# The gates of one token block added in DRAM by index

## The chip, the cores and the metric

The kernel runs on one core of one Trainium2 chip. Its engines are TensorE (PE, with its weight loads shown as PEld), VectorE (DVE), ScalarE (ACT), GpSimd (POOL) and SyncE (SP); 16 DMA engines move data between DRAM and the on-chip memory, and SP, ACT and POOL issue transfers to them on a queue each. The metric is the device time of one execution in microseconds (us), smaller is better.

## The reference

One transformer layer for 1024 tokens of width 1024. The first half is a gated mixer and its projections. The second half is PEER: every token picks 16 of 16384 experts in each of 8 heads, by the best 16 sums of two key scores, and adds up those experts' rows.

```
i1, i2: places of the 16 best scores of each half (128 keys each)
idx   = i1 * 128 + i2 of the 16 best sums
gate  = softmax(top_s)                          # per token and head, 16 numbers
act   = gelu(expert_u[idx] . h)
y     = sum over heads and choices of gate * act * expert_v[idx]
```

Nothing of what is computed changes here.

## The kernel before

The 1024 tokens are eight blocks of 128. Blocks 0 to 2 are stream A, blocks 3 to 7 are stream B (`NT` = 640 tokens). Stream A computes PEER **sparsely**: POOL gathers for each of 384 slots (block, head, choice) the 128 rows that the 128 tokens name, once from `expert_u` and once from `expert_v`, 512 KB each (line 746), and DVE takes a dot product (`u_row`, line 1139) or adds the weighted row (`v_row`, line 1148). These 768 gathers are listed in `ROWS`, spread over the units of stream B's work, and each goes to a row buffer of a small ring (`BUFFERS`); a gather waits until DVE has used the row that was in its buffer.

Stream B computes PEER **densely**, in units that run in the order of the table `UNITS`:

- 64 **E units** (`E`,0 to 63; 128 x 2 experts each in two feature tiles): PE multiplies the unit of `expert_u` with the 640 tokens, 96 matmuls of 320 columns, since every value is split in a high and a low half-precision part; ACT applies gelu and stores the result in DRAM (`a_dram`, line 990). ACT and DVE convert the next weight units (`make_hi`, line 753; `make_lo`, line 1043); DVE also ranks stream B's scores in units 0 to 35 and takes gathered rows.
- 64 **W units**, two for each of 32 groups: SP reads back `a_dram` and the gates `g_dram` (`load_group`), DVE multiplies them (`product`, line 1510), splits the product, and PE multiplies with `expert_v`.

The gates must lie densely for the product: for each token a 128 x 128 matrix over (i1, i2), mostly zero. **Spreading** makes it: beside each of the 20 E units from `E_SPREAD` = 40 to 59, for 32 tokens a unit in 8 steps of 4 tokens, DVE builds one-hot matrices (`onehot_keys`, line 1496, and `onehot_gate`, line 1503), PE multiplies them (8 matmuls of 128 columns a step, line 1925), ACT copies the outcome and stores 2 MB to `g_dram` (line 986). Ahead of it stand, on DVE, `shift_scores` in unit 35 and `gates` in unit 37; the index matrices are transposed on PE and copied out by ACT in units 38 and 39 (`index_tiles`, `indices_out`); `idx_t` closes unit 39 on DVE, **behind** that unit's gathered rows. From then on PE's next step waits on DVE, four steps at most apart.

In the loop over `UNITS` POOL, ACT, DVE and PE each work in program order. A gather's two ends are the semaphores `row_in` (landed) and `row_used` (taken by DVE). ACT's `gelu_dots` waits for the dots of two sections before. DVE's `make_lo` in an E unit that doesn't spread waits for the ACT conversion that follows this same unit's evacuation.

Of the kernel before, what the change touches and what calls it, by code (L numbers as in the profile page):

```python
# [45 lines left out]
HB = NT // 2  # L46
NGRP = 32
# [128 lines left out]
X_G = X_IDX + 6  # L176
X_END = X_G + NT // 4

# [12 lines left out]
N_SPREAD = NT // 32  # L191
E_SPREAD = 2 * NGRP - N_SPREAD - 4

# [105 lines left out]
def trunk_layer(nc, x, c_row, w_cond, b_col, w_front, ln_g, ln_b, w_spat, b_spat, conv_w,  # L299
                ln1_g, ln1_b, keys_t, u_units, v_units, u_rows, v_rows, ln2_g, ln2_b, out):  # L300
    with ExitStack() as ctx:
# [38 lines left out]
        idx_sp = sb("idx_sp", [P, SLOTS], U32)  # L340

# [94 lines left out]
        keys_t16 = zone(15300, 640, F16).rearrange("p (n c t) -> p n c t", c=2, t=2)  # L436
        gates16 = zone(15940, 640, F16).rearrange("p (n c t) -> p n c t", c=2, t=2)
        g_t = zone(16580, 640)
# [9 lines left out]
        G_t = [z.rearrange("p (n h j t) -> p n h j t", n=NT // 32, h=2, j=4) for z in (zone(5120, 5120), hB_flat)]  # L448
# [17 lines left out]
        g_dram = nc.dram_tensor("g_dram", [NGRP // 2, P, NT // 32, 2 * P], F32).ap()  # L466
# [22 lines left out]
        row_in = [sem(f"row_in{i}") for i in range(18)]  # L489
        end_in = sem("end_in")  # L490
# [72 lines left out]
        def _(sp):  # L563
# [152 lines left out]
        def _(pool):  # L716
# [4 lines left out]
            pool.iota(iota_i[:, :], pattern=[[1, P]], base=0, channel_multiplier=0).then_inc(ident_ready, 1)  # L721
            for i in range(2):
                pool.wait_ge(ws_in, 16 * (i + 1))
                pool.memset(ws_t[64:P, :, 0:64], 0.0).then_inc(mask_ready, 1)
# [5 lines left out]
            for m, (table, slot, _) in enumerate(ROWS):  # L730
# [20 lines left out]
        def _(act):  # L751
# [76 lines left out]
            def indices_out(lo, hi):  # L828

                for i in range(lo, hi):  # L830
                    kind, (first, last) = i // 2, SPLIT["B"][i % 2]
                    a = X_IDX + i
                    n, at = (last - first) * P, slice(first * P, last * P)
                    wait_x(act, a)
                    if kind < 2:
                        pairs = slice(first * P // 2, last * P // 2)
                        activation(keys_t16[:, pairs, kind, :], psX[a % 4][:, 0:n].rearrange("p (n t) -> p n t", t=2)
                                   ).then_inc(x_free[a % 4], 1)
                    else:
                        activation(g_t[:, at], psX[a % 4][:, 0:n], ACT.Copy, GS).then_inc(x_free[a % 4], 1)  # L840
# [23 lines left out]
            for n, (x, kind, u) in enumerate(UNITS):  # L864
# [69 lines left out]
                elif kind == "E":  # L934
# [18 lines left out]
                    for j in range(2):  # L953
                        for half in range(2):
# [3 lines left out]
                            if u == E_SPREAD - 1 and 2 * j + half == 1:  # L958
                                indices_out(4, 6)
# [18 lines left out]
                if (x, kind, u) == ("B", "E", E_SPREAD - 2):  # L978
                    act.wait_ge(row_used, RANK_ROWS)
                    indices_out(0, 4)  # L980
# [14 lines left out]
                if (x, kind, u) == ("B", "E", E_SPREAD - 4):  # L995
# [31 lines left out]
        def _(dve):  # L1027
# [160 lines left out]
            dve.wait_ge(ident_ready, 2)  # L1188
# [282 lines left out]

            ranks = {}
# [7 lines left out]
            def idx_t():  # L1480
                for i in range(4):
                    a = X_IDX + 5 - i
# [22 lines left out]
            def product(g):  # L1505
                dve.wait_ge(a_in[g % 2], 16 * (g // 2 + 1))
                dve.wait_ge(g_in[g // 2 % 2], 16 * (g // 4 + 1))
                for j in range(4):
                    a = A_t[g % 2][:, j, :].rearrange("p (n t) -> p n t", n=NT // 32)
                    ins = V.scalar_tensor_tensor(a, a, AS, G_t[g // 2 % 2][:, :, g % 2, j, :], ALU.mult, ALU.mult)  # L1510
                    if j < 3:
                        step(ins)
                    else:
                        settle()
                        ins.then_inc(prod_ready, 1)
# [11 lines left out]
            for n, unit in enumerate(UNITS):  # L1527
# [69 lines left out]
                elif kind == "E" and u < E_SPREAD - 4:  # L1597
# [110 lines left out]
        def _(pe):  # L1708
# [140 lines left out]
            def index_tiles(lo, hi):  # L1849

                for i in range(lo, hi):
                    flat = (i1_all, i2_all, s_all)[i // 2]["B"].rearrange("p b h k -> p b (h k)")
                    first, last = SPLIT["B"][i % 2]
                    ps = x_tile(X_IDX + i)
                    for b in range(first, last):
                        ins = nc.tensor.transpose(ps[:, (b - first) * P:(b - first + 1) * P], flat[:, b, :], ident[:, :])
# [6 lines left out]
            for n, (x, kind, u) in enumerate(UNITS):  # L1863
# [66 lines left out]
                elif (x, kind, u) == ("B", "E", E_SPREAD - 1):  # L1930
                    def gates_between(r, s):
                        if (r, s) == (1, 2):
                            pe.wait_ge(gate_ready, 2)
                            index_tiles(4, 6)
# [5 lines left out]
                if (x, kind, u) == ("B", "E", E_SPREAD - 2):  # L1940
                    pe.wait_ge(s_shift, 2)
                    index_tiles(0, 4)
# [85 lines left out]
```

## Time and profile before

| | us |
|---|---|
| median of 3 runs | 2945.51 |
| lowest and highest run | 2930.32, 2946.67 |
| span of the profiled execution | 2939.3 |
| PE, DVE, ACT, POOL busy in it | 2830.0, 2512.5, 885.5, 1029.0 |

The profiled execution is told by its span, from the first instruction to the last; its own time outside the profile is not listed, and the span lies between the lowest run and the median. A busy share over the whole span mixes stages with different limits. The E units of this trace begin near 1060 us, spreading is from 1691 to 2036 us, the W units run from about 2110 us. Granted clock 1.00 means 2.4 GHz.

### The profile page before, as it was taken

Reading aid. Unit: us, or ns where it says so; the run is one execution under the profiler, and the core shown is the slowest. Engines: PE = TensorE matmul, PEld = TensorE weight load, DVE = VectorE, ACT = ScalarE, POOL = GpSimd, SP = SyncE. Lnnn points to the kernel's source line nnn. Section 1 sums busy time; section 2 is a strip of 40 time slices with the busy share of each in tenths; the row PEclk is TensorE's granted clock in tenths of the full one; section 3 lists DMA queues with packets and bytes.
Section 4 is the critical chain, followed back from the end, with each engine's and each line's share of the span. In section 5 each row is a group of like instructions: output and inputs, shape, how many; then the busy total and the mean of one; then the engine's idle time right before and its main releaser. Section 6 shows DMA issues by size and latency. Waiting matters only on the chain. (4 is left out here: it accounts for less than half of the span.)

```text
span 2939.3 us, 47358 instructions
## 1 busy us (share of the span) xinstructions
PE 2830.0 (96%) x19184; PEld 1834.9 (62%) x19184; DVE 2512.5 (85%) x4708; ACT 885.5 (30%) x1321; POOL 1029.0 (35%) x778
## 2 busy tenths in 40 slices
PE   4999999998999999999999999999999999999998
PEld 4566686766667877677776677777544444444443
DVE  6876556987887879999999999998699999999877
ACT  3333532221111432222222344444222222222223
POOL 0000000002776025444554532222456566655410
PEclk9999999999999999999999999999999999999999
DMA  8989653433999458888888999999999999999972
GB/s 328 348 318 381 238 199 129 144 123 115 391 392 378 192 215 288 303 325 314 330 315 320 354 327 346 350 346 341 368 398 405 405 388 414 407 401 404 364 267 115
DMA packets 222971, 917.54 MB, mean 312 GB/s; under 512 B 20208, under 2 KB 61216, under 8 KB 181536
## 3 DMA queue, kind: packets, MB, share of 16 engines
q1 hardware_dynamic: 61664, 427.91, 37.3%
q0 software_dynamic: 110592, 402.70, 36.4%
q10 hardware_dynamic: 50496, 83.89, 7.9%
q8 instruction: 152, 2.49, 0.3%
q14 instruction: 67, 0.55, 0.1%
HBM read 771.79 MB, written 142.63 MB: 311 GB/s over the span
## 5 line engine op out<-in xcount | busy, mean ns | idle before, releaser
L1718 PE MATMUL psU<-hB,w 128*128 128x320 f16 (+2 forms) x3104 | 927.4, 299 | 27.4 <-ACT Z L753 15.9
L1719 PE MATMUL psU<-hB,w 128*128 128x320 f16 (+2 forms) x3104 | 927.3, 299 | 0.0
L1720 PE MATMUL psU<-hB,w 128*128 128x320 f16 (+2 forms) x3104 | 927.0, 299 | 0.0
L753 ACT ACTIVATE w<-stage 128x2048 f16<-128x2048 f32 x176 | 335.7, 1909 | 606.1 <-PE psX L1720 331.2
L1043 DVE SCALAR_TENSOR_TENSOR w<-stage,w 128x2048 f16<-128x2048 f32 x176 | 402.3, 2287 | 99.4 <-ACT w L753 99.4
L746 POOL DMA_INDIRECT rows<-in_u_rows,idx_sp x200 | 267.8, 1339 | 376.0 <-DVE rows L1139 233.5
L1718 PEld LDWEIGHTS psU<-hB,w 128*128 128x128 f16 x3104 | 304.9, 98 | 140.2 <-issue 22.9
L1720 PEld LDWEIGHTS psU<-hB,w 128*128 128x128 f16 x3104 | 305.1, 98 | 117.6
L1719 PEld LDWEIGHTS psU<-hB,w 128*128 128x128 f16 x3104 | 305.0, 98 | 110.4
L746 POOL DMA_INDIRECT rows<-in_v_rows,idx_sp x205 | 271.4, 1324 | 285.4 <-DVE rows L1139 184.5
L1718 PE MATMUL psX<-w,Z 128*128 128x512 f16 x768 | 292.2, 381 | 7.6 <-DVE Z L1641 4.2
L1719 PE MATMUL psX<-w,Z 128*128 128x512 f16 x768 | 292.6, 381 | 0.0
L1720 PE MATMUL psX<-w,Z 128*128 128x512 f16 x768 | 292.5, 381 | 0.0
L1148 DVE SCALAR_TENSOR_TENSOR acc_sp<-rows,weight_sp,acc_sp 128x1024 f32<-128x1024 f32 x205 | 258.3, 1288 | 30.5 <-DMA rows<-in_v_rows,idx_sp 26.2
L1718 PE MATMUL psU<-w,Z 128*128 128x512 f16 (+1 forms) x768 | 265.1, 345 | 5.4 <-ACT acc_sp L753 2.8
L1139 DVE SCALAR_TENSOR_TENSOR rows<-rows,h_sp 128x1024 f32<-128x1024 f32 x200 | 239.6, 1220 | 29.8 <-DMA rows<-in_u_rows,idx_sp 28.9
L1719 PE MATMUL psU<-w,Z 128*128 128x512 f16 (+1 forms) x768 | 265.1, 345 | 0.0
L1720 PE MATMUL psU<-w,Z 128*128 128x512 f16 (+1 forms) x768 | 265.0, 345 | 0.0
L753 ACT ACTIVATE R<-psU 128x320 f32<-128x320 f32 (+1 forms) x296 | 123.1, 427 | 333.6 <-PE psU L1720 333.3
L753 ACT ACTIVATE Z<-psU 128x320 f32<-128x320 f32 (+3 forms) x228 | 97.0, 445 | 383.6 <-PE psU L1720 341.6
L1718 PE MATMUL psU<-Z,w 128*128 128x384 f16 (+1 forms) x640 | 206.5, 323 | 5.6 <-DVE w L1043 5.6
L1720 PE MATMUL psU<-Z,w 128*128 128x384 f16 (+1 forms) x640 | 206.8, 323 | 0.0
(263 smaller groups left out, 4435.8 us busy)
## 6 DMA issues: line engine op xcount, KB each, us to landing
stage<-in_u_units SPq DMA_DIRECT2D x64, 1024.0 KB, 8.8
stage<-in_v_units SPq DMA_DIRECT2D x64, 1024.0 KB, 8.0
stage<-in_w_front SPq DMA_DIRECT2D x48, 1024.0 KB, 8.6
hl_dram<-w SPq DMA_DIRECT2D x48, 1024.0 KB, 6.5
w<-hl_dram SPq DMA_DIRECT2D x48, 1024.0 KB, 7.2
a_dram<-R ACTq DMA_DIRECT2D x64, 640.0 KB, 8.0
g_dram<-Z ACTq DMA_DIRECT2D x20, 2048.0 KB, 10.7
Z<-a_dram SPq DMA_DIRECT2D x32, 1280.0 KB, 11.8
```

The costliest lines, as they stand in the source:

```text
L746: pool.indirect_dma_start(row_at[r], None, u_rows if table == "u" else v_rows, bass.IndirectOffsetOnAxis(ap=idx_sp[:, slot:slot + 1], axis ...
L753: return nc.scalar.activation(dst, src, func, scale=scale)
L1043: V.scalar_tensor_tensor(w[:, n % NW, 1, :], stage[:, v % 2, :], WS, w[:, n % NW, 0, :], ALU.mult, ALU.subtract).then_inc(lo_done, 1)
L1139: V.scalar_tensor_tensor(row_at[r], row_at[r], 1.0, h2_sp[:, slot % SB, :], ALU.mult, ALU.mult, accum_out=dots[:, c % 8, j:j + 1]).then_in ...
L1148: V.scalar_tensor_tensor(dst, row_at[r], weight_sp[:, slot:slot + 1], dst, ALU.mult, ALU.add).then_inc(row_used, 1)
L1718: mm(ps, lhs[0](k), rhs[0](k), start=start and s == 0, stop=False)
L1719: mm(ps, lhs[0](k), rhs[1](k), start=False, stop=False)
L1720: last = mm(ps, lhs[1](k), rhs[0](k), start=False, stop=stop and s == n - 1)
```

## The change

Block 7, the last of stream B (`DS` = 1), is taken out of the spreading. Its gates go to a second DRAM tensor, `gs_dram` (16384 x 128 numbers, 8 MB), which is first filled with zeros: POOL clears one row buffer at the start, and ACT issues 16 transfers of 512 KB from it, one beside each of the 16 units from (`B`,`V`,2) on. When `gates` is through, DVE works out in `scatter_slots` where each gate of block 7 goes, and POOL adds the gates there: one indirect DMA with an add for each of 8 heads x 16 choices, each for 128 tokens with one number of 4 bytes a token, 128 DMAs. They stand two ahead of each gathered row, beginning with unit 38's rows; ahead of each head's 16 POOL waits until all adds before have landed, as two heads can name the same expert.

The spreading holds 512 tokens in 16 E units, 44 to 59 (`E_SPREAD` = 44); the units 40 to 43 are plain. Rank, `shift_scores` and `gates` stay where they were (`E_RANK` = 36). As `_sections` goes by `E_SPREAD - 4`, units 37 and 39 take 3 + 3 gathered rows where they took 2 + 2, and two slots leave the W units. The transposed index tiles are 3 of 512 columns where they were 6. Each pair of W groups reads 2 MB of `g_dram` and 512 KB of `gs_dram`, the latter in 1024 pieces of 512 bytes; `product` is four operations of 512 columns and one of 4 x 128.

```diff
+DS = 1
+DV = DB - DS
+NV = DV * P
+TS = DS * P
...
-N_SPREAD = NT // 32
+N_SPREAD = NV // 32
 E_SPREAD = 2 * NGRP - N_SPREAD - 4
+E_RANK = 36
+ZERO_FIRST, ZERO_N = N_OF["B", "V", 2], 16
+N_SCATTER = DS * HEADS * TOPK
+SCATTER_FIRST, SCATTER_LAST = E_RANK + 2, 2 * NGRP - 6
...
+                    sp.dma_start(G_s[pair % 2].rearrange("p h j t -> p (h j) t"), gs_dram[pair]
+                                 ).then_inc(g_in[pair % 2], 16)
...
+            sp.wait_ge(gs_added, 16 * N_SCATTER)
             load_group(0)
...
+            def add_gates(n):
+
+                for _ in range(min(n, N_SCATTER - added[0])):
+                    i = added[0]
+                    if i == 0:
+                        pool.wait_ge(scatter_ready, 1)
+                    elif i % (DS * TOPK) == 0:
+                        pool.wait_ge(gs_added, 16 * i)
+                    pool.indirect_dma_start(gs_flat, bass.IndirectOffsetOnAxis(ap=at_s[:, i:i + 1], axis=0),
+                                            gate_s[:, i:i + 1], None, compute_op=ALU.add).then_inc(gs_added, 16)
+                    added[0] += 1
+
+            pool.wait_ge(gs_zeroed, 16 * ZERO_N)
+            for m, (table, slot, c) in enumerate(ROWS):
+                _, kind, u = SEC_UNITS[c]
+                if kind == "E" and SCATTER_FIRST <= u < SCATTER_LAST:
+                    add_gates(2)
...
+                if ZERO_FIRST <= n < ZERO_FIRST + ZERO_N:
+                    if n == ZERO_FIRST:
+                        act.wait_ge(zeros_ready, 1)
+                    part = gs_zero[n - ZERO_FIRST]
+                    act.dma_start(part, zeros.unsqueeze(1).to_broadcast([P, part.shape[1], D])).then_inc(gs_zeroed, 16)
...
+            def scatter_slots():
+
+                for b in range(DS):
+                    i1, i2 = (t["B"][:, DV + b].rearrange("p h k -> p (h k)") for t in (i1_all, i2_all))
+                    step(V.tensor_scalar(i1, i1, float(TS), tok[:, b:b + 1], ALU.mult, ALU.add))
+                    settle()
+                    step(V.scalar_tensor_tensor(i2, i2, float(P * TS), i1, ALU.mult, ALU.add))
+                    settle()
+                    at = at_s[:, b * P:(b + 1) * P]
...
+                        V.tensor_copy(at, i2).then_inc(scatter_ready, 1)
...
-                dve.wait_ge(g_in[g // 2 % 2], 16 * (g // 4 + 1))
+                dve.wait_ge(g_in[g // 2 % 2], 32 * (g // 4 + 1))
                 for j in range(4):
-                    a = A_t[g % 2][:, j, :].rearrange("p (n t) -> p n t", n=NT // 32)
-                    ins = V.scalar_tensor_tensor(a, a, AS, G_t[g // 2 % 2][:, :, g % 2, j, :], ALU.mult, ALU.mult)
...
+                    a = A_t[g % 2][:, j, 0:NV].rearrange("p (n t) -> p n t", t=32)
+                    step(V.scalar_tensor_tensor(a, a, AS, G_t[g // 2 % 2][:, :, g % 2, j, :], ALU.mult, ALU.mult))
+                a = A_t[g % 2][:, :, NV:NT]
+                ins = V.scalar_tensor_tensor(a, a, AS, G_s[g // 2 % 2][:, g % 2], ALU.mult, ALU.mult)
...
-                elif kind == "E" and u < E_SPREAD - 4:
+                elif kind == "E" and u < E_RANK:
...
-                if kind == "E" and u == E_SPREAD - 5:
+                if kind == "E" and u == E_RANK - 1:
                     rank_some("B", 7, 9)
                     shift_scores("B")
-                if kind == "E" and u == E_SPREAD - 3:
+                if kind == "E" and u == E_RANK + 1:
                     gates("B", 2)
+                    scatter_slots()
```

POOL's order at unit 38, before (each row a gather; `in_u_rows` and `in_v_rows` are the expert tables, in brackets the semaphores waited for):

```order
L746 DMA Z<-in_u_rows,idx_sp 128x1024 [waits x_ready]
L746 DMA rows<-in_u_rows,idx_sp 128x1024 [waits row_used]
L746 DMA rows<-in_v_rows,idx_sp 128x1024 [waits row_used] x2
L746 DMA rows<-in_u_rows,idx_sp 128x1024 [waits row_used]
L746 DMA Z<-in_u_rows,idx_sp 128x1024 [waits row_used]
```

and in the changed kernel, from unit 38's first row to the first wait for the adds:

```order
L768 DMA gs_dram<-Z 2097152x1 [waits scatter_ready]
L768 DMA gs_dram<-Z 2097152x1
L792 DMA Z<-in_u_rows,idx_sp 128x1024 [waits row_used]
L768 DMA gs_dram<-Z 2097152x1 x2
L792 DMA rows<-in_u_rows,idx_sp 128x1024 [waits row_used]
L768 DMA gs_dram<-Z 2097152x1 x2
L792 DMA rows<-in_v_rows,idx_sp 128x1024 [waits row_used]
...
L768 DMA gs_dram<-Z 2097152x1 [waits gs_added]
L768 DMA gs_dram<-Z 2097152x1
L792 DMA rows<-in_v_rows,idx_sp 128x1024 [waits row_used]
```

Line 768 is the add, line 792 the gather. Where POOL issued one DMA a gathered row it now issues three, for 64 rows, and seven times one of them waits for the landing of those before.

DVE's order in unit 37 and at the start of unit 38, changed kernel (line 1508 to 1512 are `gates`, 1187 a dot, 1196 a weighted row):

```order
L1512 TENSOR_TENSOR Z<-Z 128x640 [waits dve_step]
L1525 TENSOR_SCALAR Z<-Z,tok 128x128 [waits gate_ready]
L1527 SCALAR_TENSOR_TENSOR Z<-Z 128x128 [waits dve_step]
L1533 CAST Z<-Z 128x128 [waits dve_step]
L1187 SCALAR_TENSOR_TENSOR rows,dots<-rows,h_sp 128x1024 [waits row_in2]
L1187 SCALAR_TENSOR_TENSOR rows,dots<-rows,h_sp 128x1024 [waits row_in3]
L1187 SCALAR_TENSOR_TENSOR rows,dots<-rows,h_sp 128x1024 [waits row_in0]
L1196 SCALAR_TENSOR_TENSOR acc_sp<-rows,weight_sp,acc_sp 128x1024 [waits row_used,row_in1,weight_ready]
```

The three operations of `scatter_slots` stand ahead of the unit's rows; the unit has a third dot and a third weighted row.

## Rows read from the trace of the kernel before

**Rows 1.** The page: busy time, and the span in 40 slices.

```profile
PE 2830.0 (96%) x19184; PEld 1834.9 (62%) x19184; DVE 2512.5 (85%) x4708; ACT 885.5 (30%) x1321; POOL 1029.0 (35%) x778
...
POOL 0000000002776025444554532222456566655410
...
DMA  8989653433999458888888999999999999999972
```

**Rows 2.** Windows: stretch, length, busy us (instructions) by engine, clock, DMA share, GB/s.

```profile
1600.00:1700.00 100.00, 90.98 (x653) 64.98 (x654) 92.89 (x166) 34.26 (x58) 53.67 (x40) 0.93 0.87 326
1700.00:1800.00 100.00, 99.31 (x942) 75.79 (x941) 99.20 (x144) 45.48 (x82) 30.18 (x26) 1.00 0.97 351
```

**Rows 3.** Tile `g_dram`: ACT's stores, duration ns, first and last start.

```profile
L986 ACTq DMA_DIRECT2D g_dram<-Z x20: 377/377/380, 1710.7 to 2035.6; - x20
```

**Rows 4.** Timeline of ACT, units 60 to 63: start, length, stores of `a_dram`.

```profile
2049.11 0.33 ACTq L990 DMA_DIRECT2D a_dram<-R  x1
...
2088.03 0.33 ACTq L990 DMA_DIRECT2D a_dram<-R  x1
```

**Rows 5.** Groups by form, DVE, 1700 to 2050 us: count, busy us, mean ns, idle before.

```profile
L1503 DVE TENSOR_TENSOR Z<-Z 128x1024 f16<-128x1024 f16 x156 | 107.4, 688 | 2.7
L1496 DVE TENSOR_TENSOR Z<-Z 128x1024 f16<-128x1024 f16 x155 | 106.0, 684 | 0.0
L1043 DVE SCALAR_TENSOR_TENSOR w<-stage,w 128x2048 f16<-128x2048 f32 x20 | 45.7, 2283 | 3.9 <-ACT w L753 3.9
L1148 DVE SCALAR_TENSOR_TENSOR acc_sp<-rows,weight_sp,acc_sp 128x1024 f32<-128x1024 f32 x28 | 35.7, 1279 | 0.0
L1139 DVE SCALAR_TENSOR_TENSOR rows<-rows,h_sp 128x1024 f32<-128x1024 f32 x28 | 34.1, 1218 | 0.0
```

**Rows 6.** Timeline of DVE at the end of unit 39.

```profile
1685.03 1.23 DVE L1139 SCALAR_TENSOR_TENSOR rows<-rows,h_sp 128x1024 f32<-128x1024 f32 x1 [3.21 <-DMA rows<-in_u_rows,idx_sp]
...
1689.93 0.48 DVE L1485 CAST Z<-Z 128x640 f16<-128x640 f32 x1
```

**Rows 7.** Timeline of PE at the first step of the spreading.

```profile
1692.99 1.04 PE L1925 MATMUL psX<-Z 128*128 128x128 f16 x8 [6.65 <-DVE Z L1503]
```

**Rows 8.** Timeline of POOL, plain units, then spreading: start, length, idle before.

```profile
1601.61 1.68 POOL L746 DMA_INDIRECT Z<-in_u_rows,idx_sp  x1 [13.84 <-DVE Z L1139]
1603.59 0.94 POOL L746 DMA_INDIRECT Z<-in_v_rows,idx_sp  x1 [0.30 <-issue]
...
1608.56 1.89 POOL L746 DMA_INDIRECT rows<-in_u_rows,idx_sp  x1 [0.31 <-issue]
...
1725.61 1.14 POOL L746 DMA_INDIRECT rows<-in_u_rows,idx_sp  x1 [2.58 <-DVE acc_sp L1148]
```

**Rows 9.** Waits, 1500 to 2060 us: total, times, longest.

```profile
POOL rows L746 <- DVE rows L1139: 116.1, 37, 13.5
POOL rows L746 <- DVE acc_sp L1148: 95.7, 29, 4.8
```

**Rows 10.** Tile `rows`, 1600 to 1700 us: time from issue to landing.

```profile
DMA to landing us min/median/max: 5.3/8.9/13.5
```

**Rows 11.** Tile `rows`, 1700 to 2050 us: the same.

```profile
DMA to landing us min/median/max: 4.5/8.2/11.9
```

**Rows 12.** The page: DMA queues, packets, MB, share of 16 engines.

```profile
q0 software_dynamic: 110592, 402.70, 36.4%
q10 hardware_dynamic: 50496, 83.89, 7.9%
```

**Rows 13.** Windows of the zero fill's units and of the W units.

```profile
440.00:540.00 100.00, 100.00 (x707) 69.55 (x706) 71.99 (x266) 25.70 (x46) 0.00 (x0) 1.00 0.40 137
540.00:620.00 80.00, 80.00 (x578) 56.99 (x577) 75.14 (x336) 22.13 (x38) 0.00 (x0) 1.00 0.30 107
...
2200.00:2300.00 100.00, 100.00 (x465) 45.25 (x464) 95.97 (x105) 24.81 (x16) 65.07 (x43) 1.00 1.00 403
```

**Rows 14.** Groups by form, 1700 to 2400 us: `product` of the W units.

```profile
L1510 DVE SCALAR_TENSOR_TENSOR Z<-Z 128x640 f32<-128x640 f32 x28 | 21.1, 815 | 13.1 <-DMA Z<-g_dram 13.1
```

More of the change, by code:

```diff
@@ L434, in trunk_layer @@
         a_ring = v3(R1[:, :], 4)
-        keys_t16 = zone(15300, 640, F16).rearrange("p (n c t) -> p n c t", c=2, t=2)
-        gates16 = zone(15940, 640, F16).rearrange("p (n c t) -> p n c t", c=2, t=2)
-        g_t = zone(16580, 640)
+        keys_t16 = zone(15300, NV, F16).rearrange("p (n c t) -> p n c t", c=2, t=2)
+        gates16 = zone(15940, NV, F16).rearrange("p (n c t) -> p n c t", c=2, t=2)
+        g_t = zone(16580, NV)
+        at_s = zone(R2 + 13968 + NV, TS, U32)
+        gate_s = zone(R2 + 14608 + NV, TS)
+        zeros = rows[:, 3, :]
         iota_k2 = v3(zone(17220, 128, F16), P)
@@ L446, in trunk_layer @@
         A_t = [v3(zone(2560 * i, 2560), 4) for i in range(2)]
-        G_t = [z.rearrange("p (n h j t) -> p n h j t", n=NT // 32, h=2, j=4) for z in (zone(5120, 5120), hB_flat)]
+        G_t = [z[:, 0:8 * NV].rearrange("p (n h j t) -> p n h j t", n=NV // 32, h=2, j=4)
+               for z in (zone(5120, 5120), hB_flat)]
+        G_s = [z[:, 8 * NV:8 * NT].rearrange("p (h j t) -> p h j t", h=2, j=4) for z in (zone(5120, 5120), hB_flat)]
         c_hi = [v3(zone(10240 + 1280 * i, 1280, F16), 4) for i in range(2)]
@@ L489, in trunk_layer @@
         row_in = [sem(f"row_in{i}") for i in range(18)]
+        zeros_ready = sem("zeros_ready")
+        gs_zeroed = sem("gs_zeroed")
+        gs_added = sem("gs_added")
+        scatter_ready = sem("scatter_ready")
         end_in = sem("end_in")
@@ L721, in _ @@
             pool.iota(iota_i[:, :], pattern=[[1, P]], base=0, channel_multiplier=0).then_inc(ident_ready, 1)
+            pool.iota(tok_i[:, :], pattern=[[P, DS]], base=0, channel_multiplier=1).then_inc(ident_ready, 1)
+            pool.memset(zeros, 0.0).then_inc(zeros_ready, 1)
+            pool.wait_ge(zeros_ready, 1)
             for i in range(2):
@@ L729, in _ @@
             pool.memset(acc_sp[:, :, :], 0.0).then_inc(acc_zeroed, 1)
-            for m, (table, slot, _) in enumerate(ROWS):
+            added = [0]
+            def add_gates(n):
[13 more added lines that the diff above has]
+                    add_gates(2)
                 r, before, _ = PLACES[m]
@@ L828, in indices_out @@
             def indices_out(lo, hi):
[L830 to L833, printed above, removed]
+                for kind in range(lo, hi):
+                    a = X_IDX + kind
                     wait_x(act, a)
                     if kind < 2:
-                        pairs = slice(first * P // 2, last * P // 2)
-                        activation(keys_t16[:, pairs, kind, :], psX[a % 4][:, 0:n].rearrange("p (n t) -> p n t", t=2)
+                        activation(keys_t16[:, :, kind, :], psX[a % 4][:, 0:NV].rearrange("p (n t) -> p n t", t=2)
                                    ).then_inc(x_free[a % 4], 1)
                     else:
-                        activation(g_t[:, at], psX[a % 4][:, 0:n], ACT.Copy, GS).then_inc(x_free[a % 4], 1)
+                        activation(g_t, psX[a % 4][:, 0:NV], ACT.Copy, GS).then_inc(x_free[a % 4], 1)
             def section_gelu(n):
@@ L1470, in slots_A @@
                 V.tensor_copy(idx_sp[:, :], idx_f).then_inc(slots_ready, 1)
+            def scatter_slots():
[6 more added lines that the diff above has]
+                    at = at_s[:, b * P:(b + 1) * P]
+                    if b < DS - 1:
+                        step(V.tensor_copy(at, i2))
+                    else:
+                        V.tensor_copy(at, i2).then_inc(scatter_ready, 1)
             ranks = {}
@@ L1480, in idx_t @@
             def idx_t():
-                for i in range(4):
-                    a = X_IDX + 5 - i
+                for a in range(X_IDX, X_G):
                     dve.wait_ge(x_free[a % 4], a // 4 + 1)
@@ L1851, in index_tiles @@
                 for i in range(lo, hi):
-                    flat = (i1_all, i2_all, s_all)[i // 2]["B"].rearrange("p b h k -> p b (h k)")
-                    first, last = SPLIT["B"][i % 2]
+                    flat = (i1_all, i2_all, s_all)[i]["B"].rearrange("p b h k -> p b (h k)")
                     ps = x_tile(X_IDX + i)
-                    for b in range(first, last):
-                        ins = nc.tensor.transpose(ps[:, (b - first) * P:(b - first + 1) * P], flat[:, b, :], ident[:, :])
+                    for b in range(DV):
+                        ins = nc.tensor.transpose(ps[:, b * P:(b + 1) * P], flat[:, b, :], ident[:, :])
                     ins.then_inc(x_ready, 1)
```

31 lines of the change are left out of this document (17 added, 14 removed).

## The prediction

> **What bounds the kernel now.** I read the windows by stage first, then the pace of the units, and only then single instructions. Over the whole span PE is busy 96% and DVE 85%, POOL 35% [rows 1]; the share says little about the stretch that the change touches. In the spreading PE and DVE are both busy 99% of each window [rows 2]. ACT stores 20 batches of gates from 1710.7 to 2035.6 [rows 3]: 324.9 / 19 = **17.1 us a spreading unit**. Three plain units behind them take 2088.03 - 2049.11 = 38.9 [rows 4], so **13.0 us a plain unit**, which is PE's own pace. DVE's list for a spreading unit, from the means [rows 5], is 8 x (0.69 + 0.68) + 2.28 + 2 x 1.28 + 2 x 1.22 = 18.2 us by busy times that overlap a little: it fills the 17.1. In a plain unit DVE has only 2.28 + 2.56 + 2.44 = 7.3 us of it.
>
> The other thing to see is the seam. The spreading starts when DVE has taken unit 39's rows and built the first one-hots: DVE waited 3.21 us there for a gathered row and came to `idx_t` at 1689.93 [rows 6], and PE stood 6.65 us [rows 7]. **Whatever makes DVE late before the seam is paid by PE at the seam**, since nothing lies between them there. And DVE is late when gathered rows are. Today POOL waits for DVE (116.1 + 95.7 us over the stretch, for buffers [rows 9]), not DVE for POOL.
>
> **What is taken away.** Four units go from spreading to plain: 4 x (17.1 - 13.0) = **-16.4 us**. Fewer index tiles are copied; they are behind PE's work and cost nothing. This is all that the change can give back, 0.6% of the time.
>
> **What is added on POOL.** 128 adds by index, each for 128 tokens like a gather. No add is in the trace. Its nearest row is the gather: 0.94 us and 0.30 to the next when nothing is waited for, with a longer one of 1.89 closing a run [rows 8]. Five issues after the run's first (0.94 x 4 + 1.89, and 5 x 0.30) make 7.15 us, **1.43 us each**; in the spreading 1.14 + 0.30 = 1.44. I take 1.43 for both kinds, as each makes descriptors for 128 indices. Ends: 0.30, if an add cost nothing but the gap, and 2.19 (1.89 + 0.30), if each was like the longest of the run. Less than nothing is excluded, since nothing leaves POOL's queue.
>
> Seven times POOL also waits until all adds have landed. A gather lands 8.9 us (5.3 to 13.5) after issue in the plain units and 8.2 (4.5 to 11.9) in the spreading [rows 10, 11]. An add stands behind the gather issued just before it, so I take 7 us, less the one gather that POOL still issues between: 7.0 - 1.4 = **5.6 us a wait**; ends 0 and 12 - 1.4 = 10.6. The rule that speaks for less: the Trainium skill, "DMA: Bandwidth & Descriptors", section "Anatomy of one DMA", puts a small transfer at about 2 us to landing, most of it the receipt of the write. By that the seven waits would cost 7 x 0.6, some 35 us less in all. The trace does not agree for this load, as no gather landed in under 4.5 us; 512 KB and the queue before it explain that.
>
> **Plain units 38 to 43.** They take 4, 6, 4, 4, 4, 4 = 26 gathered rows and so 52 adds: 78 issues x 1.43 = 111.5, and three waits (before adds 17, 33 and 49) 16.8, together 128.3 us of POOL. PE needs 6 x 13.0 = 78.0. POOL now gets there **50.3 us late**. Buffers for 5 to 7 rows cannot hide it: DVE uses a row 8 or 9 us after issue at best, and POOL itself can't start until `scatter_ready` in unit 37. I set what the buffers hide against that late start. PE runs on to the seam with weights converted up to four units ahead, and waits there.
>
> **Spreading units 44 to 53.** The other 76 adds with 38 rows, in ten units of 40: 116 x 1.43 = 165.9, and four waits 22.4, are 188.3 us against 10 x 17.1 = 171.0: **+17.3 us**. POOL is then the bound here too, by little. From unit 54 on the queue is as before.
>
> **What else moves, at nothing.** The zero fill, 8 MB, goes out beside work where DMA share is 0.40 and 0.30 [rows 13]; at the gathers' price (36.4% of 2939.3 us for 402.7 MB [rows 12] is 2.66 us a MB) it needs 22 us of some 200 that are free. POOL's memset and ACT's 16 issues wait for nobody. `scatter_slots` is three operations of 128 columns, below 0.69 us each [rows 5], in a unit where DVE's 2.28 + 3 x 1.28 + 3 x 1.22 = 9.8 us leave 3.2 for them and for `gates`. The two extra rows each in units 37 and 39 are in the count above.
>
> In the W units `product` grows from 4 x 0.815 [rows 14] to five operations of 512 columns; with the 0.815 scaled by columns at best, 0.65, it is 3.3 us, at worst 4.1: up to 0.8 us a group. A group is 10 tiles of 12 matmuls and 465 matmuls pass in 100 us [rows 13], so it lasts 25.8 us. DVE is busy 96% and PE 100% there [rows 13], so 1 us a group is about free; cost zero, at worst 32 x 0.8 less that slack, near zero. The DMA side is the thinner cover: share 1.00 at 403 GB/s. The moved 8.4 MB come in 512-byte pieces. ACT's queue, half of it in 1 KB pieces, pays 7.9% of the span for 83.9 MB [rows 12], 2.77 us a MB against 2.66, so I take nothing; if short pieces cost double it is +22 us over 32 groups.
>
> **Sum.** -16.4 + 50.3 + 17.3 = **+51 us**. Against the profiled span, 2939.3, that is 2990; the median of the runs lies 6 us above the span, so the forecast is **2996 us**.
>
> **Rivals.**
> 1. *POOL's idle time takes it all* (the other side: not slower). POOL is idle 65% of the span [rows 1] and 70% of a spreading window [rows 2]. It holds if an issue is so cheap that 52 of them with three waits, beside 26 gathers at 1.43, fit in 78.0: (78.0 - 37.2 - 3w) / 52, which is 0.78 us an add with no wait and 0.46 with the 5.6. Then only -16.4 is left: **2929**. For it: an add moves 4 bytes a token and not 4096. Against it: a gather's 0.94 us on POOL is its issue, not its transfer, which lands 8 us later. The same page of the Trainium skill calls descriptor generation "small, variable", which would put it here; the 0.94 speaks against. Chance 0.2.
> 2. *Adds land slowly.* Each engine must read, add and write 8 single numbers an add. If it does that one after the other, a wait is not 5.6 but 15 us or more, and gathers queued behind adds come late too. 7 x (15 - 5.6) = 66 more: **3062**; with 1.9 us issues (52 + 76 adds x 0.76 = 97 more) about **3160**. Nothing in the trace shows an adding DMA. Chance 0.2.
> 3. *The W units become bound by DMA*, with POOL's cost as in 1: -16.4 + 22 = **2951**. For it: DMA share 1.00; against it: PE never stands. Chance 0.05.
> 4. *The change doesn't do what it says*, if adds stay behind to the last: they'd end by unit 53 or 54 by the count, ten units before `load_group` asks. Chance 0.02.
>
> My forecast has 0.53, as far as from 2960 to 3060.
>
> **Numbers.** A measurement of this kernel tells 1%, some 29 us, from no change. Faster by over 1% would need 13 us more than the change can give: 0.06, out of rival 1's chance, for what I don't see. Within 1%, 2916 to 2975: the rest of rival 1, rival 3, and the forecast's cheap end (issues of 1.24 us and waits of 2.6: -16.4 + 26.5 + 0 = +10 us): 0.27. Slower: 0.67. The range leaves out the far end of rival 2 and little below rival 1: **2926 to 3100**.
>
> **What would show it.** The stretch of spreading has 16 stores at 17 to 19 us. POOL, 50% busy in 1600 to 1700 now, is busy or waiting for its own adds nearly throughout units 38 to 53, and its waits for DVE's buffers vanish there. DVE waits for gathered rows tens of us in all. PE stands at the seam by some 50 us, not 6.65. The W units keep 25.8 us a group. If PE's stand at the seam is below 10 us, the POOL term is wrong; if POOL is idle and still the rows are late, it is the landing.

## The result and the profile after

The change costs 5.5%: **3099.79 us**, median of 6 runs (3086.07 to 3106.52), against 2945.60 (2925.06 to 2947.60) for the kernel before in the same session, a ratio of 1.0546 (1.0511 to 1.0580). The forecast was 2996, +51 us; the measured +154 is three times that, and the time lies 0.2 us inside the upper end of the range, 3100. Of all runs told of here one, of experiment 11, was in the slower state (3003.16 us at a granted clock of 0.942, where the others of its kernel have 0.984 to 0.993) and is left out.

Where the 161.6 us between the two profiled spans lie is read off the starts of ACT's stores to `a_dram`, one an E unit:

| stretch | before | after | difference |
|---|---|---|---|
| start to unit 36 | 1645.7 | 1650.7 | +5.0 |
| unit 36 to 43 (plain units, half of the seam) | 116.7 | 117.7 | +1.0 |
| unit 43 to 44 (rest of the seam) | 17.1 | 80.7 | +63.6 |
| unit 44 to 53 (adds beside the spreading) | 153.9 | 223.9 | +70.0 |
| unit 53 to 63 | 154.7 | 154.4 | -0.3 |
| unit 63 to the end | 851.3 | 873.5 | +22.2 |

A unit's time is counted here from the store before it to its own. The kernel before has its own seam in the second row (unit 40, 25.5 us) and spreads in the units 40 to 59, so the rows compare the whole stretch better than single units. From unit 54 on the pace is 17.1 us a unit again, to the tenth.

The page after: busy time, then POOL's, the clock's and the DMA engines' 40 slices, then POOL's queue.

```profile
PE 2837.4 (92%) x18925; PEld 1827.6 (59%) x18925; DVE 2479.6 (80%) x4680; ACT 867.1 (28%) x1286; POOL 1284.6 (41%) x908
...
POOL 0000000005762144454557878852265656565520
PEclk9999999999999999999999769999999999999999
DMA  8989654337997478888888657889899999999973
...
q0 software_dynamic: 129024, 402.78, 36.4%
```

Against [rows 1] POOL has 130 instructions more and 256 us more of busy time, 7s and 8s in the slices of units 38 to 53; the same slices are where DMA is less busy than before and the clock falls. 128 of the 130 are the adds. They move 0.08 MB in 18432 packets [rows 12].

The windows of the stretch, columns as in [rows 2]:

```profile
1600.00:1700.00 100.00, 92.53 (x664) 65.89 (x665) 84.79 (x180) 32.16 (x51) 62.59 (x43) 0.95 0.83 300
1700.00:1800.00 100.00, 44.28 (x319) 31.39 (x317) 30.70 (x35) 14.71 (x24) 82.47 (x52) 0.73 0.63 158
1800.00:1900.00 100.00, 50.26 (x409) 36.75 (x410) 55.03 (x78) 19.45 (x34) 79.28 (x52) 0.74 0.64 167
```

In 1700 to 1800 every engine but POOL is idle more than half of the time, and POOL's 82.47 us with 52 gaps of 0.30 leave it no more than 2 us of waiting. That is an engine that is full, though its busy share reads 82%. How it fills, from POOL's timeline in the changed kernel:

```profile
1785.14 2.54 POOL L768 DMA_INDIRECT gs_dram<-Z  x1 [0.30 <-issue]
1787.99 1.56 POOL L768 DMA_INDIRECT gs_dram<-Z  x1 [0.30 <-issue]
1789.85 1.01 POOL L792 DMA_INDIRECT rows<-in_u_rows,idx_sp  x1 [0.30 <-issue]
1791.16 1.58 POOL L768 DMA_INDIRECT gs_dram<-Z  x1 [0.30 <-issue]
1793.05 1.56 POOL L768 DMA_INDIRECT gs_dram<-Z  x1 [0.30 <-issue]
1794.91 1.48 POOL L792 DMA_INDIRECT rows<-in_v_rows,idx_sp  x1 [0.30 <-issue]
```

One gathered row now takes two adds of 1.6 and a gather of 1.0 to 1.5, with three gaps: 5.1 us from gather to gather here, and 2 x 2.08 + 1.64 = 5.8 in the mean over the list (an add and a gather with their gaps), where PE's plain units want a row every 13.0 x 6 / 26 = 3.0. The same by groups, POOL, 1500 to 2250 us (count, busy us, mean ns, idle before):

```profile
L768 POOL DMA_INDIRECT gs_dram<-Z x128 | 227.4, 1776 | 45.4 <-issue 37.8 <-DMA gs_dram<-Z 5.2 <-DVE Z L1533 2.4
L792 POOL DMA_INDIRECT rows<-in_u_rows,idx_sp x53 | 70.0, 1320 | 64.2 <-DVE acc_sp L1196 37.6 <-DVE rows L1187 15.9 <-issue 10.7
```

An add takes 1.78 us of POOL and 0.30 to the next. The waits for the landing of adds are 5.2 us in all, in three places; at the other four all had landed when POOL came there. One of the three, the last add of a head, the gather behind it and the add that waits:

```profile
1763.94 1.56 POOL L768 DMA_INDIRECT gs_dram<-Z  x1 [0.30 <-issue]
1765.80 1.01 POOL L792 DMA_INDIRECT rows<-in_u_rows,idx_sp  x1 [0.30 <-issue]
1769.09 1.58 POOL L768 DMA_INDIRECT gs_dram<-Z  x1 [2.28 <-DMA gs_dram<-Z]
```

What the rest of the machine does meanwhile, from the waits of 1600 to 2250 us (total, times, longest):

```profile
ACT Z L799 <- PE psX L1986: 254.2, 100, 59.4
PEld psX L1986 <- DVE Z L1565: 130.5, 34, 67.6
PE psX L1986 <- DVE Z L1565: 118.8, 14, 67.1
...
DVE rows L1187 <- DMA rows<-in_u_rows,idx_sp: 59.2, 13, 8.2
...
DVE Z L1187 <- DMA Z<-in_u_rows,idx_sp: 34.4, 8, 7.2
...
PE psU L1780 <- ACT R L799: 29.7, 2, 19.9
```

Read from the bottom up: DVE waits for rows that have not come, PE waits for the one-hots that DVE makes behind those rows (line 1565 after is line 1503 before). The two timelines at the seam show each link. DVE:

```profile
1821.45 1.28 DVE L1196 SCALAR_TENSOR_TENSOR acc_sp<-rows,weight_sp,acc_sp 128x1024 f32<-128x1024 f32 x1 [4.30 <-issue]
1827.08 1.28 DVE L1196 SCALAR_TENSOR_TENSOR acc_sp<-rows,weight_sp,acc_sp 128x1024 f32<-128x1024 f32 x1 [4.34 <-DMA rows<-in_v_rows,idx_sp]
1828.28 0.15 DVE L1209 SCALAR_TENSOR_TENSOR weight_sp<-dots,gate_sp 128x2 f32<-128x2 f32 x1
1828.35 0.42 DVE L1547 CAST Z<-Z 128x512 f16<-128x512 f32 x1
```

and PE:

```profile
1761.58 0.43 PE L1780 MATMUL psU<-hB,w 128*128 128x320 f16 x1 [19.86 <-ACT R L799]
...
1763.67 0.47 PE L1782 MATMUL psU<-hB,w 128*128 128x320 f16 x1
1831.21 1.04 PE L1986 MATMUL psX<-Z 128*128 128x128 f16 x8 [67.06 <-DVE Z L1565]
```

DVE takes a row every 5.5 us, at once when it lands, and comes to `idx_t` at 1828.35, where it stood at 1689.93 before [rows 6]. PE stands 19.86 + 67.06 = 87 us, where it stood 6.65 [rows 7]. ACT, the releaser of the first of the two, was itself held by `act.wait_ge(row_used, ...)` ahead of the index copies, until DVE had taken a row:

```profile
1759.94 0.60 ACT L799 ACTIVATE Z<-psX 128x512 f16<-128x512 f32 x1 [11.65 <-DVE acc_sp L1196]
```

### The profile page after: what moved, and what is told of

Its sections match the earlier page's. It is cut to its first block and busy times, and to the rows that moved or that the text cites. A ratio compares the mean times of both kernels' runs of the same rounds, so it can differ in the third digit from the quotient of the medians.

```text
span 3100.9 us, 46894 instructions
## 1 busy us (share of the span) xinstructions
PE 2837.4 (92%) x18925; PEld 1827.6 (59%) x18925; DVE 2479.6 (80%) x4680; ACT 867.1 (28%) x1286; POOL 1284.6 (41%) x908
## 5 line engine op out<-in xcount | busy, mean ns | idle before, releaser
L792 POOL DMA_INDIRECT rows<-in_v_rows,idx_sp x207 | 279.9, 1352 | 215.6 <-DVE rows L1187 138.3
L768 POOL DMA_INDIRECT gs_dram<-Z x128 | 227.4, 1776 | 45.4 <-issue 37.8
L799 ACT ACTIVATE Z<-Z 128x2560 f16<-128x2560 f32 (+2 forms) x49 | 94.9, 1952 | 417.5 <-DVE Z L1574 370.6
L1780 PE MATMUL psU<-Z,w 128*128 128x384 f16 (+1 forms) x640 | 207.1, 324 | 3.8 <-DVE w L1091 3.8
```

The costliest lines, as they stand in the source:

```text
L768: pool.indirect_dma_start(gs_flat, bass.IndirectOffsetOnAxis(ap=at_s[:, i:i + 1], axis=0), gate_s[:, i:i + 1], None, compute_op=ALU.add).t ...
L792: pool.indirect_dma_start(row_at[r], None, u_rows if table == "u" else v_rows, bass.IndirectOffsetOnAxis(ap=idx_sp[:, slot:slot + 1], axis ...
L799: return nc.scalar.activation(dst, src, func, scale=scale)
L1780: mm(ps, lhs[0](k), rhs[0](k), start=start and s == 0, stop=False)
```

## The experiments

Each ratio is to runs of the kernel before on the same chip, whose medians were 2951.5 to 2955.8 us; "the stretch" is from unit 36's store to unit 63's in the profiled execution, 442.3 us before and 576.7 after, and "the end" what follows unit 63, 851.3 and 873.5. What lies ahead of unit 36 differs by up to 25 us between profiled executions of kernels that are the same there (1648.0 to 1672.8), so the stretch tells more than the whole time.

### 1. No adds

```diff
 if kind == "E" and SCATTER_FIRST <= u < SCATTER_LAST:
-    add_gates(2)
+    pass
...
-sp.wait_ge(gs_added, 16 * N_SCATTER)
+sp.wait_ge(gs_zeroed, 16 * ZERO_N)
```

> The changed kernel without its 128 adds; block 7's gates stay zero, so its dense share of the output is left out. Zero fill, second gate tensor, five-part product and the 16 spreading units stay. Theory (the adds' time on POOL makes the stretch from unit 36 to 63 139 us longer): all of that goes, and the four units' gain of 16 us shows there: units 36 to 63 take about 426 us against 442 before; the W units keep their loss of some 22 us; in all 0 to +10 us against before. Rival (fewer steps but a slower seam or slower plain units, whatever POOL does): the stretch stays over 450 us.

Measured: 2954.09 us, ratio 0.9999 (0.9974 to 1.0024); the stretch 423.7, the end 876.4. PE at the seam, from the waits of 1600 to 1760 us:

```profile
PE psX L1986 <- DVE Z L1565: 4.0, 1, 4.0
```

So 153 of the stretch's 576.7 us are the adds, all of them; everything else that the change does to the stretch is worth -18.6 (16.4 were forecast), and the end, 25.1 longer than before, pays it back. DVE takes unit 38's first row, the first with adds ahead of it in the changed kernel, and unit 54's first, the first behind them, 222.1 us apart here

```profile
1689.74 1.22 DVE L1187 SCALAR_TENSOR_TENSOR Z<-Z,h_sp 128x1024 f32<-128x1024 f32 x1
...
1911.80 1.22 DVE L1187 SCALAR_TENSOR_TENSOR rows<-rows,h_sp 128x1024 f32<-128x1024 f32 x1
```

and 375.2 us in the changed kernel:

```profile
1683.96 1.22 DVE L1187 SCALAR_TENSOR_TENSOR Z<-Z,h_sp 128x1024 f32<-128x1024 f32 x1
...
2059.19 1.23 DVE L1187 SCALAR_TENSOR_TENSOR rows<-rows,h_sp 128x1024 f32<-128x1024 f32 x1 [5.70 <-DMA rows<-in_u_rows,idx_sp]
```

The difference is 153.1 us: the whole loss of the stretch arises between these two rows.

### 2. A write by index in place of the add

```diff
-gate_s[:, i:i + 1], None, compute_op=ALU.add)
+gate_s[:, i:i + 1], None)
```

> The 128 indexed DMAs write instead of add (where two heads name one expert only the last is kept; that sum is left out). If the adding makes the issue longer (1.58 us and more, where a gather's is 0.94 at least), an issue falls to about 0.94 and the kernel gains 128 x 0.6, some 70 to 80 us, to about 3025 us. If it is the direction (an index on the destination, pieces of 4 bytes), the issue stays at 1.6 to 1.8 us and the time at 3090 to 3105.

Measured: 3051.82 us, ratio 1.0342 (1.0281 to 1.0402), the stretch 511.2. POOL's group, 1500 to 2250 us:

```profile
L768 POOL DMA_INDIRECT gs_dram<-Z x128 | 155.1, 1212 | 46.2 <-issue 37.8 <-DMA gs_dram<-Z 6.0 <-DVE Z L1533 2.4
```

A write by index costs POOL 1.21 us in the mean and an add 1.78. Those 0.56 us x 128 = 72 us of POOL shortened the stretch by 65.5. The expectation, 3025 us, was right that a write is cheaper, and 27 us short in size. Half of the writes take 0.985 us or less, near the gather's cheapest 0.94 (the median add takes 1.58), but longer ones raise the mean, and the queue is still the bound.

### 3. Half of the adds

```diff
-N_SCATTER = DS * HEADS * TOPK
+N_SCATTER = DS * HEADS * TOPK // 2
```

> Only the first 64 adds (four of the eight heads' gates of block 7; the other four are left out), two ahead of each row from unit 38 on, so they end near unit 45. Theory of POOL's time: the late start at the seam stays nearly whole (52 adds stand before it), the slow spreading units 46 to 53 become 17.1 us ones: about 60 us less than the changed kernel, some 3040 us. Rival (a cost per add on the DMA side that is spread evenly): half of 139, 70 us less. Rival (a fixed cost of having the adds at all): no change.

Measured: 3055.81 us, ratio 1.0355 (1.0260 to 1.0450; the two runs lie 38 us apart, so I go by the trace), the stretch 517.5, 59 less. PE stood 68.1 us at the seam as before the halving, and units 46 to 59 ran at 17.1. The two amounts that were expected, 60 us and 70, are too near each other for these runs; what speaks against a cost spread evenly over the adds is where the 59 us went: the seam kept its loss, which depends on the 52 adds ahead of it, and the rest depends on the other 76.

### 4. The adds thinned out over the units from 38 on

```diff
-if kind == "E" and SCATTER_FIRST <= u < SCATTER_LAST:
-    add_gates(2)
+if kind == "E" and u >= SCATTER_FIRST:
+    add_gates(1 if u < E_SPREAD else 1 + m % 2 if u < E_SPREAD + N_SPREAD else 2)
```

> All 128 adds, thinner: one ahead of each row in units 38 to 43, one or two by turns in the spreading units, two in unit 60. Theory (POOL's list for a unit against the unit's length): plain 4 x 1.45 + 4 x 2.0 = 13.8 against 13.0, spreading 4 x 1.45 + 6 x 2.0 = 17.8 against 17.1, so near the unit's own pace: PE's stand at the seam falls from some 60 us to 10 to 20, units 36 to 63 take 435 to 455 us, the kernel 2965 to 2985. Rival (each add costs the same wherever it stands, by its transfer on the DMA engines): the stretch stays near 577 us and the kernel near 3100.

Measured: 3047.14 us, ratio 1.0337 (1.0286 to 1.0389), the stretch 522.2: a miss by 67 us and more. PE's stand at the seam fell to 37 us, but the spreading units behind it, 46 to 59, took 21.0 us each. POOL's group shows why:

```profile
L768 POOL DMA_INDIRECT gs_dram<-Z x128 | 233.7, 1826 | 60.0 <-issue 36.9 <-DMA gs_dram<-Z 18.6 <-DVE Z L1533 4.6
```

I had filled each unit to about 17 us of POOL by the cheap prices. At 1.83 + 0.30 an add, 1.40 + 0.30 a gather (the mean in units 46 to 59) and another 1.2 us a unit of waits for landing, the list for six adds and four gathers is 20.8 us, as long as the units turned out.

### 5. Long pieces for the W units

The gates of block 7 are laid out so that a group pair's 512 KB are read in 4 KB pieces; the index is formed accordingly. By an exchange of `i1` and `i2` in that index the gates are added at other places than they should be, at the same cost (1.76 us an add).

```diff
-gs_dram = gs_flat.rearrange("(g j p t) o -> g p j (t o)", g=NGRP // 2, j=8, p=P)
+gs_dram = gs_flat.rearrange("(g p j t) o -> g p (j t o)", g=NGRP // 2, j=8, p=P)
...
```

> The changed kernel with gs_dram laid out as group, partition, expert, token, so that a pair of W groups reads it in 128 pieces of 4 KB and not 1024 of 512 bytes; three to four more small operations on DVE in unit 37 for the index. Theory A (the W units are 22 us longer because of the short pieces): DVE's waits for gs_dram, 73 us in the changed kernel, all but go and the kernel is 15 to 22 us faster, about 3080. Rival B (the fifth operation of product, or a second transfer on the queue as such): no change there, 3100.

Measured: 3083.25 us, ratio 1.0426 (1.0402 to 1.0451), the end 854.5 and not 873.5, the stretch 576.7 as in the changed kernel. The W units' waits for the gates, 2150 to 3050 us, in the changed kernel

```profile
DVE Z L1572 <- DMA Z<-gs_dram: 44.7, 7, 17.9
...
DVE Z L1572 <- DMA hB<-gs_dram: 28.6, 7, 5.7
```

and with long pieces

```profile
DVE Z L1580 <- DMA Z<-gs_dram: 14.5, 1, 14.5
```

Of 14 waits one is left, and 19 us went with the others, while the fifth operation of `product` and the second transfer stayed. PE in 2400 to 2500 us is busy 96.17 us with short pieces and 100.00 with long ones:

```profile
2400.00:2500.00 100.00, 96.17 (x444) 42.85 (x442) 92.30 (x106) 22.58 (x14) 59.49 (x39) 1.00 1.00 389
```

```profile
2400.00:2500.00 100.00, 100.00 (x465) 45.37 (x464) 95.91 (x109) 24.81 (x16) 59.14 (x44) 1.00 1.01 401
```

### 6. The last two together

```diff
-    add_gates(2)
+    add_gates(1 if u < E_SPREAD else 1 + m % 2 if u < E_SPREAD + N_SPREAD else 2)
...
-gs_dram = gs_flat.rearrange("(g j p t) o -> g p j (t o)", g=NGRP // 2, j=8, p=P)
+gs_dram = gs_flat.rearrange("(g p j t) o -> g p (j t o)", g=NGRP // 2, j=8, p=P)
```

> The thinner adds and the layout in long pieces together. If both theories hold, the two gains add: 2945 to 2970 us, about the time before, since 16 us are given by the four units and POOL's list is still a little over a unit's length. If the W loss is not the pieces, it stays 20 us above that.

Measured: 3034.94 us, ratio 1.0288 (1.0254 to 1.0322), the stretch 522.0 and the end 856.3 (the index is experiment 5's). The time missed the expected 2945 to 2970 by 65 us, as experiment 4's did. The two effects add up: the stretch is experiment 4's and the end within 2 us of experiment 5's, as they lie in different stages.

### 7. No add ahead of the seam

```diff
-SCATTER_FIRST, SCATTER_LAST = E_RANK + 2, 2 * NGRP - 6
+SCATTER_FIRST, SCATTER_LAST = E_SPREAD, 2 * NGRP - 4
```

> The changed kernel with all 128 adds in units 44 to 59, behind the seam, two ahead of each row. Theory (POOL's time a unit): units 38 to 43 run at 13.0 us and the seam is as before, 6 to 7 us, but all 16 spreading units last 24 to 25 us where now nine of them do: units 36 to 63 take 426 + 16 x 7.5 = 546 us against 577, the kernel about 3070. Rival (the loss is one at the seam, in the row buffers): nearly all of it goes, 2970.

Measured: 3075.02 us, ratio 1.0406 (1.0364 to 1.0448), the stretch 533.9 (546 was expected). Units 38 to 43 ran at 13.2, PE's longest stand in the spreading was 6.6 us, and units 45 to 59 took some 24.5 each. The loss is not the seam's: it goes wherever POOL's list is longer than the unit. It is 43 us smaller here than in the changed kernel; the adds now stand against sixteen units of 17.1 us and none of 13.0.

### 8. The adds in the rank's units

```diff
-if kind == "E" and SCATTER_FIRST <= u < SCATTER_LAST:
-    add_gates(2)
+if kind == "E" and u >= 1 and m % 4 != 3:
+    add_gates(1)
...
```

> The 128 adds moved into units 1 to about 34, ahead of three of every four gathered rows, and long pieces in the W units. The gates aren't ready there, so the adds put zeros at fixed places as widely spread as the real ones; block 7's gates are left out. Theory (an add costs 2.0 to 2.1 us of POOL wherever it stands, and what counts is POOL's list for a unit): about 5 gathers x 1.6 + 3.75 adds x 2.1 = 15.9 us against units of 16.8 us on average, so nearly all is hidden: units 36 to 63 take 424 us as without adds, units 0 to 36 at most 20 us more than before, the kernel 2930 to 2960. Rival (the DMA engines' work on the adds is what costs): units 0 to 36 grow by 100 us or more, 3030 and over.

Measured: 3012.08 us, ratio 1.0210 (1.0135 to 1.0286). The stretch is 422.9, as without adds, but the units 0 to 36 took 646.1 us and not 571.9: +74, where 20 at most were expected, and 100 or more by the rival that the DMA engines' work on the adds is what costs: neither came true. Windows of this kernel and, behind it, of the kernel before:

```profile
1200.00:1300.00 100.00, 85.57 (x589) 59.85 (x588) 78.85 (x219) 22.69 (x41) 81.34 (x55) 0.89 0.85 271
```

```profile
1200.00:1300.00 100.00, 97.03 (x706) 69.57 (x704) 95.57 (x273) 29.18 (x52) 53.07 (x40) 0.98 0.85 314
```

POOL again reads 81% with 55 gaps of 0.3, which is full. The chain is another one: ACT waits for the dots of late rows, and PE for ACT. Over 1100 to 1650 us:

```profile
ACT dots L802 <- DVE rows L1190: 75.0, 12, 15.8
...
ACT dots L802 <- DVE Z L1190: 52.0, 11, 17.0
```

The first of the two was 8.2 us in 4 times before, and PE's waits for ACT (`psU` for `R`) went from 7.2 us to 44.8. No stage of the E units that was tried has room for 128 adds. Against the rival speaks that the DMA share in this window is 0.85 in both kernels, while POOL has no room left in the one with the adds.

### 9. Half of the indices in each add

```diff
-ap=at_s[:, i:i + 1], axis=0), gate_s[:, i:i + 1]
+ap=at_s[0:64, i:i + 1], axis=0), gate_s[0:64, i:i + 1]
```

> The changed kernel with each of the 128 adds for 64 tokens only; the gates of block 7's other 64 tokens are left out. If an add's time on POOL goes with its indices (descriptors), the issue falls from 1.58 us towards 0.8 to 0.9 and the kernel by 128 x 0.7, to about 3010. If it is a price for the instruction, nothing changes: 3100.

Measured: 3099.68 us, ratio 1.0483 (1.0388 to 1.0579), the stretch 562.8. An add of 64 tokens took POOL 1.63 us, one of 128 took 1.78: from 64 indices to 128 the price hardly rises, and 0.15 x 128 = 19 us of POOL went with 14 us of the stretch. Half the tokens in each add buys a tenth of the loss; fewer instructions buy more (experiment 3).

### 10. 96 adds, one a row, long pieces

```diff
-N_SCATTER = DS * HEADS * TOPK
+N_SCATTER = 3 * DS * HEADS * TOPK // 4
...
+if kind == "E" and u >= SCATTER_FIRST:
+    add_gates(1)
```

> 96 adds (six of the eight heads; the others' gates are left out), one ahead of each row from unit 38 to the end, long pieces in the W units. Theory: in a spreading unit POOL's list is 4 x 1.6 + 4 x 2.1 = 14.8 us against 17.1, so the spreading units are 17.1 us again; the plain units 38 to 43, 14.8 against 13.0, still make the seam late by 25 to 35 us as in the run with thinner adds. Units 36 to 63: about 424 + 35 = 460 us. Rival (a cost for each add on the DMA side): 96/128 of the 135 to 150 us, so 530 us.

Measured: 2985.11 us, ratio 1.0101 (1.0067 to 1.0135), the stretch 465.3 (460 was expected). With four rows and four adds a unit the spreading keeps 17.1 us; what is left is the seam, where unit 44 took 57.8.

### 11. The ceiling: no adds, long pieces

```diff
-    add_gates(2)
+    pass
...
-gs_dram = gs_flat.rearrange("(g j p t) o -> g p j (t o)", g=NGRP // 2, j=8, p=P)
+gs_dram = gs_flat.rearrange("(g p j t) o -> g p (j t o)", g=NGRP // 2, j=8, p=P)
```

> No adds at all (block 7's gates left out) and long pieces in the W units: what the change could give if its adds were free. Units 36 to 63 some 424 us against 442, W units as before: 18 us faster than before in the trace, ratio 0.993 to 0.996, 2930 to 2935 us.

Measured: 2946.56 us, ratio 0.9948 (0.9906 to 0.9991), the stretch 422.4, the end 856.0 (a ratio of 0.993 to 0.996 was expected). With adds that cost nothing at all the idea would gain half a per cent.

### 12. The whole computation at the best rate found

```diff
-    add_gates(2)
+    add_gates(1 if u < E_SPREAD else 1 + (m % 4 == 0) if u < E_SPREAD + N_SPREAD else 3)
...
```

with the layout in 4 KB pieces and the right index.

> The whole computation, all 128 adds: one ahead of each row in units 38 to 43, five for each spreading unit's four rows, three ahead of each row in units 60 and 61, long pieces in the W units. Theory (POOL's list against the unit): spreading 4 x 1.6 + 5 x 2.1 = 16.9 against 17.1, so those units stay near 17.1 and at most 18; the seam is late by the 35 us of the thin run; the last 22 adds in two plain units make these 10 to 25 us longer. Units 36 to 63: 475 to 500 us, the kernel 2995 to 3015 us. Rival (any add slows its unit, list or not): 16 units at 20 us as in the run with six adds, 515 to 525 us, 3030.

Measured: 3031.74 us, ratio 1.0255 (1.0196 to 1.0314), the stretch 508.6, the end 858. This missed the expected 2995 to 3015, and the 475 to 500 for the stretch. Units 46 to 57 took 17.1 to 21.6, 18.6 in the mean, unit 44 took 54.7 and unit 62, behind the remaining adds, three a row, 39.1. The count had 16.9 us a spreading unit; by the prices measured here, 1.86 + 0.30 an add and 1.34 + 0.30 a gather, five adds and four gathers are 17.4, and the waits for landing, which the count left out, another 1.1. It is the best version with all adds, and it doesn't beat the kernel before. The count says that none by a mere shift can: units 38 to 61 last 8 x 13.0 + 16 x 17.1 = 378 us, and POOL's list for them, at the changed kernel's prices, is 98 gathers x 1.64 + 128 adds x 2.07 = 426.

## Why the prediction was right in kind and short in size

**The mechanism held, link by link.** POOL's queue full from unit 38 to 53, rows late to DVE, DVE late to `idx_t`, PE standing at the seam, the pace of 17.1 back from unit 54: each was forecast and each is in the rows above. Taking the adds out (experiment 1) takes all of it away. The rival that POOL's idle time takes it all would have needed an add of 0.5 to 0.8 us; it took 2.08. The size was off by a factor of three: +154 us and not +51. That the time still lies in the range is luck. The range reached to 3100 for the rival in which adds land slowly, which has no support in the rows, and the measured 3099.79 lies outside the 2960 to 3060 to which the forecast itself gave 0.53.

**The step that failed is "I take 1.43 for both kinds".** POOL's list over units 38 to 53, from the first add at 1673.76 to the first gather behind the last at 2050.95, took 377 us; the prediction has 128.3 + 188.3 = 317. By its terms:

| term | forecast | measured | difference |
|---|---|---|---|
| 128 adds | 128 x 1.43 = 183 | 227.4 + 37.8 = 265 | +82 |
| the gathers among them | 66 x 1.43 = 94 | 63: 84.3 + 0.3 each = 103 | +9 |
| waits for landing | 7 x 5.6 = 39 | 5 | -34 |
| waits for DVE | 0 | 3 | +3 |

The sum of the differences is 60 us. The two large errors had opposite signs, so the sum looked better than its parts: the add was nearer to the upper bound I had written down, 2.19, than to the value I took, and the waits were nearly nothing. The argument for 1.43 was that a gather makes descriptors for as many indices; experiments 2 and 9 contradict it from two sides, since the price goes with whether the instruction adds (0.56 us) and hardly with how many indices it holds (0.15 us for 64).

**A second term was mis-sized: what the list was held against.** The prediction held POOL's list against 78.0 + 171.0 = 249.0 us of units at their own pace, and "I set what the buffers hide against that late start" put both ends of the list at nothing. Without the adds the same rows take DVE 222.1 us (experiment 1), not 249.0: it takes unit 38's first row 20.1 us behind unit 37's store and unit 54's first 13.8 us ahead of unit 53's store (1669.67 and 1925.59), so it gains on the units meanwhile. This gain is lost too when POOL's list is what DVE waits for: 375.2 - 222.1 = 153.1 us, where 316.6 - 249.0 = 67.6 were forecast. Of the 85.5 between them the longer list has 58.6 (DVE's 375.2 against 316.6) and the smaller base 26.9.

**The landing.** I took 7 us from the gathers and kept a page of the Trainium skill against it: "DMA: Bandwidth & Descriptors", section "Anatomy of one DMA", puts a small transfer at about 2 us to landing, most of it the receipt of the write. Both figures miss, from two sides. In the three waits of the changed kernel the waiting add starts 3.4 to 5.3 us behind the start of the last add before it (1763.94 and 1769.09 in the rows above), and at the other four places 3.4 to 4.4 us were enough; with adds spaced wider the waits rose to 18.6 us in 6 (experiment 4), 3.1 each, and ended 5.0 to 8.5 us behind that start. My wait had also an error in it: the 7 us run from the start of the issue, and of them I took off the gather, 1.4, but not the add's own time on POOL, another 1.4, so that by my own prices a wait was 4.1 us and not 5.6, 10 us less over seven. The same page of the Trainium skill calls descriptor generation "small, variable". No trace here splits POOL's 1.78 us an add into its parts; if they are this generation, small they are not, since they bound the stretch.

**"For short pieces I take nothing" failed too**, and the end I had priced at +22 came true: the W units lost 22.2 us, and the length of the pieces alone gets 17 to 20 of them back (experiment 5 against the changed kernel 19.0, 6 against 4 16.8, 11 against 1 20.4). The stream was at DMA share 1.00 [rows 13], so there was no cover, and the prediction had said so.

**The rest.** The gain of four plain units, with everything else that the change does to the stretch without its adds, was 18.6, not 16.4. The sum of what is named, 58.6 + 26.9 - 2.2 + 22.2 + 5.0 (ahead of unit 36, less than what moves there between kernels that are the same), is 110.5 of the 110.6 us between the forecast span, 2990.3, and the measured one. PE's granted clock was 0.50, its 1.2 GHz level, from 1745.5 to 1834.2 us, while PE stood, in the few matmuls between its two stands and in the first 3 us behind the second; its matmul of 320 columns takes 0.47 us there and 0.30 before, which makes some 3 us at most and needs no term of its own.

**What the rivals got.** That adds land slowly has no support: 5.2 us in all. Its second half, issues of 1.9 us for 97 us more, was nearly right on its own: 1.78, for 82 us more.

## What to carry to other kernels

An instruction of a kind that the trace does not hold should be priced at its upper bound on the queue that issues it, until one run shows its duration: 0.65 us more than its nearest relative, 128 times, was the largest part of the error here. An engine's idle share is no free room when its in-order queue also issues what others wait for; sum that queue's list for a unit, gaps included, and hold it against the unit's length (here 5.8 us a row against 3.0). Ask too how far the rows run ahead of the units today, as that lead is lost with it (27 us here). And a stream at DMA share 1.00 has no cover for shorter pieces.

## What the runs showed of the hardware

- POOL's time for an indirect DMA goes by its kind: a gather of 128 rows 1.0 to 2.1 us among the adds (median 1.39; 0.94 at least elsewhere), a write by index 1.21 in the mean (median 0.985), an add by index 1.78 (median 1.58; 84 of the 128 below 1.6, 14 above 2.4), with 0.30 us to the next in each case.
- It hardly goes by the indices: an add of 64 took 1.63 us, one of 128 took 1.78. Why adding costs POOL more than writing is open. The packets on its queue (the page's DMA queues) are 32 for a write of 128 numbers, 80 for an add of 64 and 144 for an add of 128; their number alone does not give the price, as the step from 80 to 144 costs 0.15 us and the one from 32 to 80 costs 0.42.
- An add moves 128 numbers in 144 packets (18432 more on the queue for 128 adds), and the DMA engines had room for them: their share in 1700 to 1800 us was 0.63, where it had been 0.97 with more gathers [rows 2].
- Where POOL waited for an add to land, the wait ended 3.4 to 5.3 us behind the start of that add in the changed kernel, and 5.0 to 8.5 us in experiment 4.
- 8 MB read in 512-byte pieces rather than in 4 KB ones cost the W units, at DMA share 1.00, 17 to 20 us.
